# Sparse attention of the prompt and of the samples in one block, and linear attention in another order, in a two-layer decoder step

## What is computed

```python
def gla_chunked(q, k, v, log_a, s0):          # chunks of 64 tokens
    def step(s, inp):
        b = jnp.cumsum(ai, axis=2)
        att = jnp.where(causal, einsum(qi * exp(b), ki * exp(-b)), 0.0)
        o = att @ vi + (qi * exp(b)) @ s
        s_new = exp(b[-1]) * s + (ki * exp(b[-1] - b)).T @ vi
...
log_a = log_sigmoid(a1 @ w_a2 + b_a2) / GLA_TAU
o_b = rms(o_b, onorm_g) * silu(rb)
...
def nsa_block(q, g, ...):
    p_c = masked_softmax(q @ kc * scale + bias_2d(dist_c), dist_c >= 0)
    imp = einsum(p_c, cover)                  # importance of each block of 64 keys
    idx = top_k(score(imp), 16)               # 17 blocks of a sample: one is dropped
    p_s = masked_softmax(q @ ks[idx] * scale + b_s, s_pos <= q_pos)
    p_w = masked_softmax(q @ kw * scale + bias_2d(dist_w), in_window)
    return g[0] * (p_c @ vc) + g[1] * (p_s @ vs[idx]) + g[2] * (p_w @ vw)
```

## Time and profile before

| what | value |
| --- | --- |
| time, median of 3 runs | 1971.27 us (1965.73 to 1981.54) |
| the profiled execution | 1977.11 us, its span 1975.5 us |
| PE busy / VectorE / ScalarE / POOL in the span | 1739.8 / 839.8 / 696.1 / 120.1 us |
| linear_attention, from its first load to its last operation | 652.3 to 720.0 us |
| qk_norms | 1358.0 to 1403.9 us |
| sparse_prompt | 1404.2 to 1551.5 us |
| sparse_sample | 1551.8 to 1693.6 us |
| memory read / written in the span | 344.69 / 15.94 MB |

### The profile page before, as it was taken

One profiled execution on the slowest core, in us unless ns is written; L12 is line 12 of the kernel. 1 busy time (PEld: TensorE's weight loads), 2 busy tenths in 40 slices (PEclk: granted clock), 3 DMA queues, 4 the chain that ended last, 5 costly groups with the idle time before them and its releaser, 6 DMA issues. The chain is left out here.

```text
span 1975.5 us, 34686 instructions
## 1 busy us (share of the span) xinstructions
PE 1739.8 (88%) x14084; PEld 1572.5 (80%) x14084; DVE 839.8 (43%) x1111; ACT 696.1 (35%) x1039; POOL 120.1 (6%) x249
## 2 busy tenths in 40 slices
PE   6999999999645679999999999998689577899998
PEld 4779999989523468999989999897567344799998
DVE  3464443452432355343354444531135256454433
ACT  4353333243322124332343333434234233343332
POOL 3310000000133000000000000000000122000000
PEclk9999999999867569999999999998558688899999
DMA  9956665453479016666344343553340355343430
GB/s 321 392 191 278 256 260 202 171 215 129 157 258 340 25 67 234 261 260 261 133 186 185 142 157 142 180 197 130 59 183 1 97 177 177 118 171 133 166 128 28
DMA packets 71563, 354.10 MB, mean 179 GB/s; under 512 B 12194, under 2 KB 35634, under 8 KB 55123
## 3 DMA queue, kind: packets, MB, share of 16 engines
q1 hardware_dynamic: 59794, 317.60, 43.3%
q0 software_dynamic: 11648, 34.81, 5.3%
HBM read 344.69 MB, written 15.94 MB: 183 GB/s over the span
## 5 line engine op out<-in xcount | busy, mean ns | idle before, releaser
L457 DVE TENSOR_TENSOR sb_Wlow<-sb_ring,sb_Whigh 128x2048 fp32r<-128x2048 f32 x136 | 311.8, 2292 | 280.4 <-ACT sb_Whigh L454 280.4
L454 ACT ACTIVATE sb_Whigh<-sb_ring 128x2048 fp32r<-128x2048 f32 x136 | 260.1, 1912 | 161.0 <-PE PS L580 158.6
L580 PE MATMUL PS<-sb_Hhigh,sb_Whigh 128*128 128x320 f32 x1360 | 231.6, 313 | 0.5 <-DVE sb_Wlow L457 0.5
L580 PE MATMUL PS<-sb_Hlow,sb_Whigh 128*128 128x320 f32 x1360 | 228.0, 310 | 0.0
L580 PE MATMUL PS<-sb_Hhigh,sb_Wlow 128*128 128x320 f32 x1360 | 227.1, 309 | 0.0
L580 PEld LDWEIGHTS PS<-sb_Hhigh,sb_Whigh 128*128 128x128 f32 x1360 | 207.3, 189 | 4.8 <-issue 3.8
L580 PEld LDWEIGHTS PS<-sb_Hlow,sb_Whigh 128*128 128x128 f32 x1360 | 207.7, 189 | 0.0
L580 PEld LDWEIGHTS PS<-sb_Hhigh,sb_Wlow 128*128 128x128 f32 x1360 | 206.4, 188 | 0.0
L677 ACT ACTIVATE sb_S<-PS 128x320 f32<-128x320 f32 x88 | 38.5, 438 | 439.6 <-PE PS L580 428.2
L731 DVE TENSOR_TENSOR sb_S<-sb_S,PS 128x320 f32<-128x320 f32 x88 | 42.9, 488 | 268.1 <-ACT sb_S L677 268.1
L580 PE MATMUL PS<-sb_Ghigh,sb_Whigh 128*128 128x320 f32 x704 | 118.9, 309 | 0.0
(11 more groups left out here) (446 smaller groups left out, 2357.3 us busy)
## 6 DMA issues: line engine op xcount, KB each, us to landing
sb_ring<-w_slots SPq DMA_DIRECT2D x119, 2048.0 KB, 7.7
sb_s_K<-sb_kT SPq DMA_DIRECT2D x32, 256.0 KB, 6.3
sb_s_K<-sb_kT POOLq DMA_DIRECT2D x32, 256.0 KB, 5.7
sb_s_V<-sb_v SPq DMA_DIRECT2D x32, 256.0 KB
sb_s_V<-sb_v POOLq DMA_DIRECT2D x32, 256.0 KB, 5.5
sb_KS<-slc_kT SPq DMA_DIRECT2D x64, 128.0 KB, 2.2
sb_C<-cmp_k SPq DMA_DIRECT2D x32, 128.0 KB, 7.5
sb_C<-cmp_k POOLq DMA_DIRECT2D x32, 128.0 KB, 6.2
```

The source lines that it names most:

```text
L454: nc.scalar.activation(Ws[0][:, b], columns, ACT.Copy).then_inc(high_done.sem, 1)
L457: nc.vector.tensor_tensor(Ws[1][:, b], columns, Ws[0][:, b], ALU.subtract).then_inc(low_done.sem, 1)
L580: mm = nc.tensor.matmul(to, Ws[w][:, b, q % KT, i, :], ins[x][:, q, :], start=(first and a == 0 and q == tiles[0]), stop=(last and a == 2 ...
```

## The change

Six edits, in the order of the program.

1. The loads of w_a2 and b_a2 are issued by SP at the start of stick_sample, into space that is free then.
2. In linear_attention, ScalarE's Silu comes first and the table of the norm is loaded behind it; VectorE expands vx while it waits for the exponentials; on TensorE the sums of squares stand ahead of the products for the states; on VectorE the output's norm stands ahead of the additions to the states.
3. The project stage of the second layer leaves two of the four ring slots unfilled, and the out stage fills them at its start. In between they hold the bias table B1 and the logits of the prompt.
4. In qk_norms SP issues the 16 loads of the bias table and the keys of sample 0 ahead of the gate rows.
5. sparse_prompt and sparse_sample become one block, sparse_both, of 9 rounds without a loop: a round has the scores of sample n+1 and of prompt batch n+1, and the values of sample n and of prompt batch n. A prompt batch is now two key heads times two groups, so that the two heads use the two halves of TensorE's array. Adding a bias and taking the maximum become one instruction on VectorE (tensor_tensor_reduce). The key scores of a sample are 6 products of 64 columns instead of 12 of 32.
6. KS, KW, VS and VW have one buffer each.

The diff, cut to its core:

```diff
                 def _(sp):
+                    for j in range(held):
+                        fetch(sp, n0 - held, 0, j)
...
-                            fetch(sp, n0, 0, j)
+                    for j in range(n - hold):
+                        sp.wait_ge(low_done.sem, low_done.at(2 * j + 2))
...
                 def _(sp):
+                    wa2, ba2 = decay_weights()
+                    sp.dma_start(wa2, io["w_a2"]).then_inc(loads.sem, 16)
+                    sp.dma_start(ba2, bass.AP(io["b_a2"].tensor, 0, [[0, P], [1, 256]])).then_inc(loads.sem, 16)
...
 
+                    pe.wait_ge(squared.sem, squared.at(5))
+                    for h in range(4):
+                        mm = nc.tensor.matmul(PS[:, h, 0:NT], ones[:], sq[:, h, :], start=True, stop=True)
+                    mm.then_inc(summed.sem, 1)
...
 
-                    pe.wait_ge(squared.sem, squared.at(5))
-                    for h in range(4):
-                        mm = nc.tensor.matmul(PS[:, h, 0:NT], ones[:], sq[:, h, :], start=True, stop=True)
-                    mm.then_inc(summed.sem, 1)
...
+                    nc.scalar.activation(rT[:], rT[:], ACT.Silu).then_inc(squared.sem, 1)
+                    norm_table()
...
                         .then_inc(exponent.sem, 1)
...
                     nc.vector.tensor_tensor(soft[:], soft[:], x[:], ALU.add).then_inc(keep_ready.sem, 1)
+                    for h in range(4):
+                        v = vb[0:64, 2, h * P:(h + 1) * P]
+                        m = in_seq[:]
+                        m = bass.AP(m.tensor, m.offset, [list(a) for a in m.ap] + [[0, P]])
+                        last = nc.vector.tensor_tensor(vx[:, h, :, :], rep(v, 1, NB), m, ALU.mult)
...
-                    dve.wait_ge(out_ready.sem, out_ready.at(7))
                     dve.wait_ge(state_in.sem, state_in.at(32))
                     for a in range(2):
                         e = EL[:, a, 4:12]
                         e = bass.AP(e.tensor, e.offset, [list(q) for q in e.ap] + [[0, P]])
                         step(nc.vector.tensor_tensor(so[:, :, a, :], S0[:, :, a, :], e, ALU.mult))
+                    dve.wait_ge(deviation.sem, deviation.at(1))
+                    step(nc.vector.tensor_tensor(rs[:], rs[:], OT[:, 4:8, :], ALU.mult))
+                    nc.vector.scalar_tensor_tensor(out=OT[:, 4:8, :], in0=rs[:], scalar=og[:, 0:1], in1=rT[:],
+                                                   op0=ALU.mult, op1=ALU.mult)
+                    dve.wait_ge(out_ready.sem, out_ready.at(7))
+                    for a in range(2):
                         for half in range(2):
                             v = so[:, 4 * half:4 * half + 4, a, :]
                             src = PS[:, 4 + 2 * a + half, :].rearrange("p (b v) -> p b v", b=4)
-                            step(nc.vector.tensor_tensor(v, v, src, ALU.add))
-                    dve.wait_ge(deviation.sem, deviation.at(1))
-                    step(nc.vector.tensor_tensor(rs[:], rs[:], OT[:, 4:8, :], ALU.mult))
-                    nc.vector.scalar_tensor_tensor(out=OT[:, 4:8, :], in0=rs[:], scalar=og[:, 0:1], in1=rT[:],
-                                                   op0=ALU.mult, op1=ALU.mult).then_inc(centred.sem, 1)
+                            last = nc.vector.tensor_tensor(v, v, src, ALU.add)
+                    last.then_inc(centred.sem, 1)
                     dve_step.count = step.n
 
...
-                    sp.dma_start(wa2[:], io["w_a2"]).then_inc(loads.sem, 16)
-                    sp.dma_start(ba2[:], bass.AP(io["b_a2"].tensor, 0, [[0, P], [1, 256]])).then_inc(loads.sem, 16)
...
-                return out_stage(1, n1, OT)
+                return out_stage(1, n1, OT, 2)
...
+                spare = [ring[:, (n1 - 2 + m) % RING, :, :].rearrange("p k n -> p (k n)") for m in range(2)]
+                B1 = spare[0].rearrange("p (h k) -> p h k", h=16)
+                zs_p = [spare[1][:, 2048 * m:2048 * m + 2048].rearrange("p (j k) -> p j k", j=8) for m in range(2)]
+
+                def load_first(sp):
+                    for a in range(16):
+                        sp.dma_start(B1[8 * a:8 * a + 8, :, :],
+                                     bass.AP(f, DIST_HI - 128 - 8 * a, [[NDIST - 1, 8], [8 * NDIST, 16], [1, 256]]))\
+                            .then_inc(table_in.sem, 16)
+                    load_keys(sp, KS, KW, pages, 0)
+                qk_norms(Q2, kskw, kcvc, vsvw, GT, GS, Bs, Bw, qkg, OT, KC, VC, load_first)
+                sparse_both(Q2, kskw, vsvw, GT, GS, Bs, Bw, KC, VC, OT, KS, KW, VS, pages, B1, zs_p)
...
+                    load_first(sp)
...
+                def load_values(eng, b, span, sig, used=None):
                     for p in span:
...
+                        page = eng.value_load(pages[0:1, b * NPG + p:b * NPG + p + 1], min_val=0, max_val=NPOOL - 1)
                         if p == span[0] and used is not None:
                             eng.wait_ge(*used)
...
-                    load(sp, 1, "keys", (page_in[1], 1))
-                    load(sp, 0, "first values", (first_values_in, 0))
-                    with sp.Fori(1, NB // 2) as g:
-                        for i in range(2):
-                            load(sp, 2 * g + i, "keys", (page_in[i], i), (logit_ready.sem, logit_ready.at(i - 1) + 2 * g))
-                            load(sp, 2 * g + (i - 1), "first values", (first_values_in, 0),
-                                 (out_ready.sem, out_ready.at(i - 1) + 2 * g))
-                    load(sp, NB - 1, "first values", (first_values_in, 0), (out_ready.sem, out_ready.at(NB - 1)))
+                    for b in range(NB):
+                        if b:
+                            load_keys(sp, KS, KW, pages, b, (s_keys.sem, s_keys.at(b)))
+                        load_values(sp, b, range(HALF), first_values_in, (s_out.sem, s_out.at(b)) if b else None)
+                        if b == 0:
+                            store(sp, io["o_wink"], io["win_k"][:, LS:WIN, :])
...
+                        for bank, keys in ((0, KS[:, 0:4]), (1, KS[:, 4:8]), (2, None)):
+                            for t in range(2):
+                                r = slice(64 * t, 64 * t + 64)
+                                nc.tensor.matmul(PS[r, bank, :], QB[:, t, r], KW[:, t, :] if keys is None else
+                                                 keys[:, :, t, :], start=True, stop=True)
...
-                    pipeline(pe, scores, values)
+                    for n in range(-1, N):
+                        nxt = n + 1
+                        if nxt < N:
+                            sample_scores(nxt)
+                            prompt_scores(nxt, 0)
+                            sample_importance(nxt)
+                        if n >= 0:
+                            sample_turns(n)
+                            prompt_turns(n)
+                            sample_values(n)
+                        if nxt < N:
+                            prompt_scores(nxt, 1)
+                        if n >= 0:
+                            prompt_values(n)
+                            sample_back(n)
...
+                    def biased(b):
+                        i, st = b % 2, stats[b % 2]
+                        dve.wait_ge(s_keys.sem, s_keys.at(b + 1))
+                        nc.vector.tensor_tensor_reduce(out=zw[i][:, WIN:NW], in0=zwn, in1=Bw[:, WIN:NW], scale=1.0,
+                                                       scalar=NEG, op0=ALU.add, op1=ALU.max, accum_out=st[:, 5:6])
+                        nc.vector.tensor_tensor_reduce(out=zw[i][:, 0:WIN], in0=zwp, in1=Bw[:, 0:WIN], scale=1.0,
+                                                       scalar=NEG, op0=ALU.add, op1=ALU.max, accum_out=st[:, 4:5])
+                        nc.vector.tensor_tensor_reduce(out=zs[i][:, PAST:NS], in0=zsn, in1=Bs[:, PAST:NS], scale=1.0,
+                                                       scalar=NEG, op0=ALU.add, op1=ALU.max, accum_out=st[:, 8:9])
+                        nc.vector.tensor_tensor(zs[i][:, 0:PAST], zsp, Bs[:, 0:PAST], ALU.add).then_inc(s_evac.sem, 1)
+
+                    def chosen_max(b):
...
-                    pipeline(dve, scores, values, step, 20)
+                    for n in range(-1, N):
+                        nxt = n + 1
+                        if nxt < N:
+                            compressed_max(nxt)
+                            prompt_max(nxt, 0)
+                            compressed_weights(nxt)
+                            biased(nxt)
+                        if n >= 0:
+                            sample_copies(n)
+                        if nxt < N:
+                            chosen_max(nxt)
+                            prompt_max(nxt, 1)
+                        if n >= 0:
+                            prompt_outs(n)
+                            sample_outs(n)
+                        if nxt < N:
+                            sample_weights(nxt)
+                            prompt_weights(nxt)
```

768 lines of the change are left out of this document (372 added, 396 removed).

## The result

The changed kernel takes 2016.95 us (median of 4 runs, 2016.74 to 2020.79) against 1973.14 us of the kernel before (4 runs, 1965.73 to 1981.54). The ratio is 1.0211, with a 95% interval of 1.0177 to 1.0245: slower, by some 42 us by the ratio where 29 were forecast, and within the stated range. The profiled execution took 2016.74 us, with a span of 2015.2 us against 1975.5.

The account below looks back on a forecast made before the run. It took SP's single in-order queue, with one buffer each, to decide the merged block's cycle. Block +34.6 and linear attention -6.5 gave +28 us: 2005 on the profiled 1977.1, 2000 on the median; range 1940 to 2035 us.

Parts of the forecast that it names:

- The mechanism: Merged block: SP's in-order queue with single buffers decides the cycle; 17 us to landed keys, TensorE idle about 11.
- From keys to values: Merged block, landed keys to last value matmul: all steps hang on one another, 24.9 us (26.4 in later cycles).
- VectorE's pause: Merged block, between scores and importance: VectorE's maxima, compressed weights and biased sample logits take 7.0 us per cycle.
- The block's start: Merged block before its first cycle: tables built, sample 0 scored, keys 1 fetched, chain run once: 48 us.
- the cover (6 us): qk_norms: moved gate loads still end before VectorE's last work, some 6 us to spare; 0 to +5, taken as 0.
- Linear attention: Linear attention: earlier weight loads and new order save 6.5 us; the end is the state's, not the norm's.
- The clock: Merged block: scores and transposes at half speed, prompt scores and most values at full; block 328, taken as 324 us.
- rival (a): Merged block: TensorE's clock stays up, block 274 us, kernel 1949 us; decides from cycles under 38 us; chance 0.22.
- (c): Sample scores: the column halves don't run at once, 5 us more in each of seven scores, 2035 us; chance 0.10.
- Rival (d): Merged block: SP isn't last, TensorE's work bounds the block at 236 us, kernel 1911 us; chance 0.08.

Follow-up runs that it names:

- key-order run: Changed kernel with SP issuing the keys of the next sample ahead of the values of this one: 1942.80 us, ratio 0.9824 to the kernel before.
- early-stores run: Changed kernel with the two window stores issued in linear_attention instead of in the merged block: 1986.33 us, ratio 1.0074 to the kernel before.
- fill kernels: Changed kernel with unread TensorE products during six key waits: 24 each, 2013.7 us; 30 in short and 26 in long cycles, 2004.63 us.
- key order, early stores and gates first: Changed kernel with next keys ahead of values, window stores in linear_attention, gate rows ahead of the bias table in qk_norms: 1909.67 us, ratio 0.9687.

## Why the prediction was right, and where it was not

**The mechanism was right.** SP, with one buffer and nothing that can pass, sets the cycle: 12.3 us of key wait in each of six cycles (forecast 11), 16.9 us from the last value product to the landed keys (forecast 17). Reordering the same issues took the wait away and 74 us with it. The Trainium skill's sentence in "DMA: Bandwidth & Descriptors", section "Issuing engines are not separate DMA queues", that issuing is usually small relative to the DMA, did not hold here: by it the cycle would have been some 13 us shorter than the rows of issue and landing make it, and the stretch from values to keys came to 16.9 us where these rows gave 17. The key-order run says it once more: with the same durations of issue, but taken out of the cycle, it was 12.6 us shorter (38.1 to 25.5).

**The block's total hides two errors.** Its parts, in us:

| part | forecast | after |
|---|---|---|
| start of the block to the end of the first values | 48 | 74.1 |
| six cycles | 255.9 | 228.7 |
| last weights, turns and values | 24 | 21.5 |
| sum | 328, taken as 324 | 324.3 |

**From keys to values I was too long, by 24 us over six cycles** (the other 3 us of the 27 lie in the waits). Forecast 24.9 and 26.4 us, measured 20.7 and 22.1 to 22.7 (the longest from 1688.96 to 1711.66). The term that failed is VectorE's pause: 7.0 us forecast, 4.29 and 4.86 measured. VectorE between the scores and the importance product:

```profile
1546.54 0.28 DVE L2909 CUSTOM_DVE_ANT_0 sb_ring<-PS,sb_ring 128x128 f32<-128x128 f32 x1
1546.74 0.08 DVE L2909 DVE_READ_ACCUMULATOR2_ANT sb_mx<- 128x1 f32 x1
1546.74 0.16 DVE L2916 CUSTOM_DVE_ANT_0 sb_zc_p<-PS,sb_ring 128x7 f32<-128x7 f32 x1
...
1546.83 0.28 DVE L2909 CUSTOM_DVE_ANT_0 sb_ring<-PS,sb_ring 128x128 f32<-128x128 f32 x1
```

A fused add-and-maximum over 128 columns and a small one come every 0.29 us: the four pairs take 1.2 us (1.8 over 256 columns) where I had 3.4 with what they leave behind, since the small ones cost 0.09 and not 0.2 to 0.3, and the accumulator's read (0.08) lies under the next operation. I took the middle of its bounds; the lower one, nothing, was right. The rest is prompt transposes at 2.0 and 3.7 us for 2.7 and 4.2, sample values at 2.1 for 2.6, and transposes at 3.2 to the next product for 3.6.

**The block's start I had too short, by 26 us.** I had the first values end 48 us after the block's start; they ended 74.1 us after it (1408.82 to 1482.94). The step that failed: I read which loads stand ahead of keys 1 on SP, but left out the two stores there, although the code has them. In the kernel before they stand on SP too, in the prompt's block, but the next load behind them comes at 1552.76, so that nothing paid for them:

```profile
1427.67 1.01 SPq L1044 DMA_DIRECT2D o_wink<-win_k  x1
```

SP in the kernel after:

```profile
1413.69 0.86 SPq L1045 DMA_DIRECT2D o_wink<-win_k  x1
1414.61 0.70 SPq L1045 DMA_DIRECT2D o_winv<-win_v  x1
1422.04 14.06 SPq L1849 DMA_DIRECT2D sb_KS<-slc_kT  x8
1436.14 19.03 SPq L1851 DMA_DIRECT2D sb_KW<-win_kT  x1
```

The stores take 1.6 us to issue and look harmless. The keys behind them take 14.06 us to issue instead of 8, and the single issue of the window keys 19.03 instead of 0.4. From 1422.04 to the landing at 1462.49 it is 40.5 us; by rows 3 I had 12.3. The two kernels that move the stores and nothing else show 4.56 us of wait in place of 33.45. Had the chain been as long as I had it, the block would have taken 350 us. Without the stores the short chain would have given 298, and the kernel would have come out near 1986, as the early-stores run did, within 1% of the kernel before.

**qk_norms I priced at nothing, and it cost 11.2 us.** I had named the cover (6 us) and the price (14.5 us of issue), and chose 0 from 0 to 5. The price was too small, too:

```profile
1356.69 21.19 SPq L1836 DMA_DIRECT2D sb_ring<-bias_rows  x16
1378.99 9.31 SPq L1849 DMA_DIRECT2D sb_KS<-slc_kT  x8
...
1389.51 1.08 SPq L2277 DMA_DIRECT2D gate_rows<-sb_GT  x1
1401.55 5.55 SPq L2282 DMA_DIRECT2D sb_GS<-gate_rows  x16
```

Sixteen table loads took 21.19 us of SP, not the 5.6 of sixteen gate loads: I took a row of the same count but of a far smaller transfer (0.8 KB each, and not 128). The table's own 32 loads took 13.53 us in the trace of before, which would have been nearer. The gate rows' store, 1.08 us to issue, then needed 10.9 us to land (8.1 before), and their loads begin 50 us after the stage's start (at 1401.55), where before it was 15 (at 1372.59). VectorE's last operation of the stage ends at 1395.80, so 13 us of the stage are loads alone. The order isn't the whole cause: with the gate rows first the stage is as long in two kernels of three (57.6 and 59.7 us). In the kernel with the old blocks, which loads the table there but no keys, it is 3.5 us longer than before.

**Linear attention: -9.3 for -6.5.** The order is as forecast, and the four state adds come last, but what they wait for isn't what I said. I had them follow the state products. These ended at 708.48, and the adds began at 710.62, behind VectorE's norm of the outputs (709.15 + 1.55): the norm's chain still sets the end, and the adds stand behind it. The term that I had wrong is the state products, 3.70 us and not the 7.14 of before, at which I had left them. Their granted clock was 0.50 before, behind 14.3 us of smaller products within 14.6 us, and 1.00 after, behind the 4.09 us of the sums of squares. Of these 3.4 us the norm let some 1.6 through; the other 1.2 of the 2.8 lie ahead, since the sums of squares were done that much sooner than forecast.

**The clock** went as chosen: scores and transposes at half speed, prompt products and most values at full, 0.68 to 0.74 over a cycle (in some of them the last scores were at full already). But the point from which I let rival (a) decide, a cycle under 38 us, was wrong: cycles of 36.9 to 37.6 us came, at 0.68 to 0.72. In the two fill kernels the clock of the scores went with the idle time ahead of them. Filled, it gave 12 us, where a block wholly at full speed was to give 50 (324 to 274); VectorE's pause stayed, and with it the transposes at half speed.

**The other rivals.** The column halves do run at once: four half-speed products of 128x64 took 3.68 us where eight of 128x32 took 3.64, so (c) falls. Rival (d), 1911 us if SP were not last, was rightly given little for this kernel. With key order, early stores and gates first SP isn't last, and that kernel takes 1909.67; that the two figures agree is chance, since (d) had a block of 236 us bounded by TensorE, and the block there takes 219.7 with TensorE busy 73% of its steady part.

**What stays open:** what decides how much clock a run with the table ahead of the old blocks gets (all but one of its runs lie within 21 us); why the sixteen table loads take 14.7 us to issue in one kernel and 21.2 in another, and with that what the order in qk_norms is worth; what brings the clock down in the fastest kernel behind short waits; and what that kernel would gain if VectorE's pause were filled.

## What to carry to other kernels

Where loads share one in-order queue and one buffer, write out for a cycle who stands behind whom: a load whose buffer is free belongs ahead of a load that still waits for its buffer, and here this order alone was worth 74 us. A big copy is paid by the loads that come next, on that queue and here on POOL's too, so put it in a stage that asks for nothing soon, and look for it in the code, since its own issue takes under a microsecond. When a load is moved, price it from its own row, issue and transfer, and not from a row with the same count of other loads; and when a total agrees, check its terms against the trace, for two errors of 26 us met here in a block that was right to 0.4.

## What the runs showed of the hardware

- An issue can itself be held up: one issue of the window keys took 19.03 us on SP behind two stores of 4,032 KB, where it takes 0.43 to 0.66 in the six cycles. What in the queue holds it no run here separates.
- Transfers that one engine asked for slow those of another: the window values that POOL had asked for took 28.6 us to land while SP's stores ran, and 4.1 to 5.0 in later cycles; SP's window keys took 26.3, and later 3.5 to 3.9:

```profile
sb_VW<-win_v POOLq DMA_DIRECT2D x1, 512.0 KB, 28.6
sb_KW<-win_kT SPq DMA_DIRECT2D x1, 512.0 KB, 26.3
```

  The Trainium skill has this in "DMA: Bandwidth & Descriptors", section "Issuing engines are not separate DMA queues": DMAs of all issuing engines end up on the same 16 DMA engines and interleave there. The trace agrees.
- TensorE's clock at the scores in the fill kernels: full speed behind pauses of up to 1.09 us, half behind 2.71 to 3.27, and full first and lower soon behind 1.73 and 2.54. The pause just ahead isn't the whole of it, though. In the fastest kernel the four key products took 3.49 us, nearly half speed, behind a wait of 0.66:

```profile
1574.76 0.63 PE L2601 MATMUL PS<-sb_KC,sb_QB 128*128 128x63 f32 x4 [0.66 <-DVE sb_OT L2898]
1575.32 3.49 PE L2610 MATMUL PS<-sb_KS,sb_QB 128*64 128x512 f32 x8
```

- VectorE's read of its accumulator takes 0.08 us and costs nothing between fused operations, where ScalarE's took 0.19.
